# A hybrid attention layer: x given a second time by columns, and the first projection by feature chunks

## The reference

```python
u = rms_norm(h, attn_pre_g)                 # h = x, 512 x 1024
proj = u @ w_in                             # w_in 1024 x 1952
c_q, c_kv, k_r = proj[:, :256], proj[:, 256:384], proj[:, 384:416]
moba_qkv = proj[:, 416:]                    # 3 x 8 heads x 64
...                                         # two attention groups of 8 heads
h = h + rms_norm(mix @ w_out, attn_post_g)
u = rms_norm(h, mlp_pre_g)
h = h + rms_norm(square(relu(u @ w_up)) @ w_down, mlp_post_g)
```

## Time and profile before

| | |
|---|---|
| median of 3 runs | 570.49 us (570.36 to 570.64) |
| the profiled execution | 570.74 us |
| its span, first to last instruction | 568.9 us |
| PE busy | 553.5 us, 97% of the span |
| DVE, ACT, POOL busy | 392.3, 297.1, 95.2 us |
| mean granted TensorE clock | 0.997 |

### The profile page before, as it was taken

One profiled execution on the slowest core, in us unless ns is written; L12 is line 12 of the kernel. 1 busy time (PEld: TensorE's weight loads), 2 busy tenths in 40 slices (PEclk: granted clock), 3 DMA queues, 4 the chain that ended last, 5 costly groups with the idle time before them and its releaser, 6 DMA issues.

```text
span 568.9 us, 8013 instructions
## 1 busy us (share of the span) xinstructions
PE 553.5 (97%) x2824; PEld 460.6 (81%) x2824; DVE 392.3 (69%) x750; ACT 297.1 (52%) x624; POOL 95.2 (17%) x157
## 2 busy tenths in 40 slices
PE   7999999999999999999999999999999999999995
PEld 6988898877666788998888888888888888888883
DVE  3539572477885436537676677569868889787897
ACT  5573153588897353535434433435445657556461
POOL 1064020254779002200000000000000001000003
PEclk9999999999999999999999999999999999999998
DMA  8451242000002661078867788678985645506403
GB/s 298 153 149 56 88 172 75 0 2 2 0 2 75 236 191 55 1 296 279 292 241 253 280 258 298 238 251 294 337 297 189 221 162 209 199 24 221 149 1 148
DMA packets 42911, 95.15 MB, mean 167 GB/s; under 512 B 3840, under 2 KB 22016, under 8 KB 39552
## 3 DMA queue, kind: packets, MB, share of 16 engines
q1 hardware_dynamic: 41840, 94.74, 47.8%
q10 hardware_dynamic: 1040, 0.00, 0.1%
HBM read 79.01 MB, written 15.73 MB: 167 GB/s over the span
## 4 chain that ended last, share of the span: by engine, by line
PE 93%; ACT 2%; DVE 2%; DMA 1%; issue 1%; SPq 0%; POOLq 0%; DVEq 0%; POOL 0%; ACTq 0%
PE bank L1346 28%; PE bank L1347 28%; PE bank L1348 28%; PE bank L1550 2%; PE bank L1571 2%; PE bank L1512 1%; ACT probs L662 1%; DMA x_sb<-in_x 1%; DVE bank L1013 1%; PE bank L1456 1%; PE bank L1352 1%; PE bank L1385 1%; DVE pT L1062 0%; ACT pT L690 0%; PE bank L1475 0%
## 5 line engine op out<-in xcount | busy, mean ns | idle before, releaser
L1346 PE MATMUL bank<-uT_hi,w_hi 128*128 128x512 f32 (+1 forms) x280 | 104.1, 372 | 0.0
L1347 PE MATMUL bank<-uT_lo,w_hi 128*128 128x512 f32 (+1 forms) x280 | 103.9, 371 | 0.0
L1348 PE MATMUL bank<-uT_hi,w_lo 128*128 128x512 f32 (+1 forms) x280 | 103.8, 371 | 0.0
L1346 PE MATMUL bank<-w_hi,a_hi 128*128 128x512 f32 x224 | 87.3, 390 | 0.0
L1347 PE MATMUL bank<-w_lo,a_hi 128*128 128x512 f32 x224 | 87.2, 389 | 0.0
L1348 PE MATMUL bank<-w_hi,a_lo 128*128 128x512 f32 x224 | 87.2, 389 | 0.0
L893 DVE SCALAR_TENSOR_TENSOR w_lo<-w_raw,g_up,w_hi 128x256 fp32r<-128x256 f32 x128 | 52.1, 478 | 47.1 <-ACT w_hi L557 47.1
L557 ACT ACTIVATE w_hi<-w_raw,g_up 128x256 fp32r<-128x256 f32 x128 | 53.0, 496 | 44.7 <-PE bank L1348 28.5
L557 ACT ACTIVATE w_hi<-w_raw 128x1024 fp32r<-128x1024 f32 (+2 forms) x49 | 46.8, 1001 | 52.5 <-PE bank L1348 48.9
L890 DVE TENSOR_TENSOR w_lo<-w_raw,w_hi 128x1024 fp32r<-128x1024 f32 (+1 forms) x41 | 48.9, 1234 | 23.2 <-ACT w_hi L557 23.1
L1346 PE MATMUL bank<-w_hi,uT_hi 128*128 128x512 f32 (+1 forms) x160 | 62.1, 388 | 0.0
(11 more groups left out here) (157 smaller groups left out, 949.1 us busy)
## 6 DMA issues: line engine op xcount, KB each, us to landing
stage<-in_w_down SPq DMA_DIRECT2D x17, 1024.0 KB, 5.0
w_raw<-in_w_up SPq DMA_DIRECT2D x16, 1024.0 KB, 8.2
pair_sums<-stage SPq DMA_DIRECT2D x13, 1024.0 KB, 9.9
w_raw<-in_w_down SPq DMA_DIRECT2D x10, 1024.0 KB, 6.9
w_raw<-pair_sums SPq DMA_DIRECT2D x10, 1024.0 KB, 4.7
w_raw<-in_w_in SPq DMA_DIRECT2D x6, 1024.0 KB, 5.8
w_raw<-in_w_out SPq DMA_DIRECT2D x4, 1024.0 KB, 4.8
stage<-pair_sums SPq DMA_DIRECT2D x3, 1024.0 KB, 4.8
```

Source lines behind the costliest of these rows:

```text
L1346: nc.tensor.matmul(out, lh, rh, start=start, stop=False)
L1347: nc.tensor.matmul(out, lh, rl, start=False, stop=False)
L1348: return nc.tensor.matmul(out, ll, rh, start=False, stop=stop)
```

## The change

- x is given a second time, transposed on the host (`x_cols`, features by tokens). Its eight chunks of 128 features by 512 tokens go to a tile `x_raw`, and ACT and DVE split them straight from there. No tile of x is transposed on PE; x in its first layout is still loaded, for the norm, later.
- Group 0 goes by feature chunk: for each k all four tiles t, three matmuls each, in four PSUM banks that stay open over all eight chunks. Chunk 0 goes pass by pass over the tiles, the others tile by tile.
- ACT splits for each k first x, then the weights; DVE first the weights, then x. The weights of group 0 come as eight loads of 208 KB, each with its own semaphore.
- ACT's queue issues the chunks 0 and 1 of x and `g_in` between them; SP issues the rest, weights and x in turn. Both gains (`attn_pre_g`, `mlp_pre_g`) are laid out on the host as the tiles want them.
- One warming block of 20 matmuls in place of 12 and 24.

```diff
+    x_cols_v = x_cols.rearrange("(k p) t -> k p t", p=P)
...
+        with ExitStack() as cols:
+            x_raw = sb("x_raw", [P, ND, S], stack=cols)
...
+        def in_rows(k, by_row, by_chunk):
+            return (by_chunk, k // 4 + 1) if k % 4 == 3 else (by_row, k - k // 4 + 1)
...
-            x_half(0, 0)
-            for i, n in ((0, first_in), (1, raw_in[0])):
-                sp.dma_start(raw[0][:, 2 * CA * i:2 * CA * (i + 1)].rearrange("p (k n) -> p k n", k=2),
-                             w_in_v[:, 2 * i:2 * i + 2, 0:CA]).then_inc(n, 16)
-            for t in range(1, NT):
-                x_half(t, 0)
-            x_half(0, 1)
-            in_chunk(1)
-            for t in range(1, NT):
-                x_half(t, 1)
+            def first_rows(k):
+                w = slice(CA * (k % 4), CA * (k % 4) + CA)
+                sp.dma_start(raw[k // 4][:, w], w_in_v[:, k, 0:CA]).then_inc(raw_in[k // 4] if k % 4 == 3 else first_in[k], 16)
+
+            for k in range(ND):
+                first_rows(k)
+                if k >= 1 and k + 1 < ND:
+                    sp.dma_start(x_raw[:, k + 1, :], x_cols_v[k + 1]).then_inc(x_cols_in[k + 1], 16)
+            in_chunk(2)
+            for t in range(NT):
+                sp.dma_start(x_sb[:, t, :], x_v[t]).then_inc(x_in[t], 16)
...
-            for i in range(2, 6):
+            for i in range(3, 6):
                 in_chunk(i)
-            sp.dma_start(g_up[:, :], mlp_pre_g[0].rearrange("(k p) -> p k", p=P), allow_slow_non_contiguous=True).then_inc(g_up_in, 16)
+            sp.dma_start(g_up[:, :], mlp_pre_g).then_inc(g_up_in, 16)
...
-            act.dma_start(g_in[:, :], attn_pre_g[0].rearrange("(k p) -> p k", p=P), allow_slow_non_contiguous=True).then_inc(g_in_in, 16)
+            act.dma_start(x_raw[:, 0, :], x_cols_v[0]).then_inc(x_cols_in[0], 16)
+            act.dma_start(g_in[:, :], attn_pre_g).then_inc(g_in_in, 16)
+            act.dma_start(x_raw[:, 1, :], x_cols_v[1]).then_inc(x_cols_in[1], 16)
...
+            def first_hi(k):
+
+                act.wait_ge(x_cols_in[k], 16)
+                hi_part(uT_hi[:, k, :], x_raw[:, k, :]).then_inc(uh, 1)
+                if k == 0:
+                    act.wait_ge(g_in_in, 16)
+                act.wait_ge(*((raw_in[k // 4] if k % 4 == 3 else first_in[k]), 16))
+                w = slice(CA * (k % 4), CA * (k % 4) + CA)
+                hi_part(w_hi[w_slot(k // 4)][:, w], raw[k // 4][:, w], g_in[:, k:k + 1]).then_inc(in_rows(k, first_h, wh_ready)[0], 1)
...
+            for k in range(ND):
+                first_hi(k)
             in_hi(2)
             for t in range(NT):
-                for b in range(2):
-                    act.wait_ge(x_in[t][b], 16)
+                act.wait_ge(x_in[t], 16)
                 square(x_sb[:, t, :], 0, t, 0)
...
+            def first_lo(k):
+                dve.wait_ge(*in_rows(k, first_h, wh_ready))
+                w, s = slice(CA * (k % 4), CA * (k % 4) + CA), w_slot(k // 4)
+                lo_scaled(w_lo[s][:, w], raw[k // 4][:, w], g_in[:, k:k + 1], w_hi[s][:, w]).then_inc(in_rows(k, first_ready, w_ready)[0], 1)
+                dve.wait_ge(uh, k + 1)
+                lo_part(uT_lo[:, k, :], x_raw[:, k, :], uT_hi[:, k, :]).then_inc(ul, 1)
...
+            def first_group():
+
+                for k in range(ND):
+                    s, w = w_slot(k // 4), slice(CA * (k % 4), CA * (k % 4) + CA)
+                    passes = ((uT_hi, w_hi), (uT_hi, w_lo), (uT_lo, w_hi))
+                    if k == 0:
+                        pe.wait_ge(first_h, 1)
+                        pe.wait_ge(uh, 1)
+                        order = [(t, n) for n in range(3) for t in range(NT)]
+                    else:
+                        pe.wait_ge(*in_rows(k, first_ready, w_ready))
+                        pe.wait_ge(ul, k + 1)
+                        order = [(t, n) for t in range(NT) for n in range(3)]
+                    for t, n in order:
+                        if k == 0 and t == 0 and n >= 1:
+                            pe.wait_ge(first_ready if n == 1 else ul, 1)
+                        x, h = passes[n]
+                        last = nc.tensor.matmul(ps[t][:, 0:CA], x[:, k, P * t:P * t + P], h[s][:, w],
+                                                start=k == 0 and n == 0, stop=k == ND - 1 and n == 2)
+                        if k == ND - 1 and n == 2:
+                            last.then_inc(proj, 1)
+                    if k == 3:
+                        last.then_inc(w_used, 1)
...
             pe.wait_ge(consts, 3)
-            warm(12)
-            group(0, before_latents)
+            warm(20)
+            first_group()
             group(1, lambda part, t: None)
...
+    arrays["x_cols"] = np.ascontiguousarray(arrays["x"][0].T)
+    for name in ("attn_pre_g", "mlp_pre_g"):
+        arrays[name] = np.ascontiguousarray(arrays[name][0].reshape(-1, P).T)
```

More of the change, by code:

```diff
@@ L33, in build @@
 def build(nc, x, attn_pre_g, w_in, mla_q_norm_g, w_mla_q_up, mla_kv_norm_g, w_mla_kv_up, w_out,
-          attn_post_g, mlp_pre_g, w_up, w_down, mlp_post_g, rope_table, out):
+          attn_post_g, mlp_pre_g, w_up, w_down, mlp_post_g, rope_table, x_cols, out):
     S, D = x.shape[1], x.shape[2]
@@ L166, in build @@
         ps = [ctx.enter_context(nc.psum_tensor(f"bank{b}", [P, TOP], F32)) for b in range(8)]
-        x_in = [[sem(f"x{t}{b}_in") for b in "lr"] for t in range(NT)]
+        x_in = [sem(f"x{t}_in") for t in range(NT)]
+        x_cols_in = [sem(f"x_cols{k}_in") for k in range(ND)]
         h_in = [sem(f"h{t}_in") for t in range(NT)]
@@ L173, in build @@
         raw_in = [sem(f"raw{i}_in") for i in range(2)]
-        first_in = sem("first_in")
+        first_in = [sem(f"first{k}_in") for k in range(ND)]
         first_h, first_ready = sem("first_h"), sem("first_ready")
@@ L561, in in_hi @@
                 r, n = IN_CH[i], GROUP_COLS[i // 2][1]
[L562 to L565, removed]
+                arrived(r)
                 for k in range(4):
[L567 to L570, removed]
                     w, kg = slice(n * k, n * k + n), 4 * (i % 2) + k
@@ L583, in square, with transposed_hi @@
                                      accum_out=stat[:, norm, t, col:col + 1]).then_inc(sq, 1)
[L585 removed]
+            def transposed_hi(t):
                 for b in range(2):
[L588 removed]
+                    act.wait_ge(uT_full, 2 * t + b + 1)
                     hi_part(uT_hi[:, 4 * b:4 * b + 4, P * t:P * t + P],
                             ps[2 * t + b][:, :].rearrange("p (k n) -> p k n", k=4)).then_inc(uh, 1)
[L592 to L608, removed]
+            for k in range(ND):
+                first_hi(k)
             in_hi(2)
             for t in range(NT):
[L611 to L612 removed]
+                act.wait_ge(x_in[t], 16)
                 square(x_sb[:, t, :], 0, t, 0)
@@ L792, in _ @@
                 if t >= 1:
-                    transposed_hi(2 * NT, t - 1)
+                    transposed_hi(t - 1)
                 if t >= 2:
@@ L796, in _ @@
             square(h_sb[:, NT - 2, :], 4, NT - 2, 0)
-            transposed_hi(2 * NT, NT - 1)
+            transposed_hi(NT - 1)
             square(h_sb[:, NT - 1, :], 4, NT - 1, 0)
@@ L897, in in_lo @@
                 r, n = IN_CH[i], GROUP_COLS[i // 2][1]
-                dve.wait_ge(*((first_h, 1) if i == 0 else (wh_ready, r + 1)))
+                dve.wait_ge(wh_ready, r + 1)
                 for k in range(4):
-                    if i == 0 and k >= 1:
-                        last.then_inc(first_ready, 1)
-                        dve.wait_ge(*((first_h, k + 1) if k < 3 else (wh_ready, 1)))
                     w, kg = slice(n * k, n * k + n), 4 * (i % 2) + k
@@ L911, in transposed_lo @@
                     lo_part(uT_lo[sl], ps[2 * t + b][:, :].rearrange("p (k n) -> p k n", k=4), uT_hi[sl]).then_inc(ul, 1)
[L913 to L927, removed]
+            for k in range(ND):
+                first_lo(k)
             in_lo(2)
@@ L1364, in group @@
                         if t == 0:
-                            pe.wait_ge(*((first_ready, 1) if r == 0 else (w_ready, r + 1)))
+                            pe.wait_ge(w_ready, r + 1)
                         tok = slice(P * t, P * t + P)
                         for k in range(4):
-                            if r == 0 and t == 0 and k >= 1:
-                                pe.wait_ge(*((first_ready, k + 1) if k < 3 else (w_ready, 1)))
                             w = slice(n * k, n * k + n)
-                            last = mm3(ps[4 * (g > 0) + t][:, 0:n], uT_hi[:, 4 * part + k, tok], uT_lo[:, 4 * part + k, tok],
+                            last = mm3(ps[4 + t][:, 0:n], uT_hi[:, 4 * part + k, tok], uT_lo[:, 4 * part + k, tok],
                                        w_hi[w_slot(r)][:, w], w_lo[w_slot(r)][:, w], part == 0 and k == 0, part == 1 and k == 3)
@@ L1376, in group @@
                         last.then_inc(w_used, 1)
[L1378 to L1386, removed]
```

3 lines of the change are left out of this document (removed).

## The result

The changed kernel takes 566.79 us (median of 4 runs, 566.40 to 567.10) against 570.49: ratio 0.9935, 95% interval 0.9923 to 0.9947, or 3.7 us faster. The forecast was 565.6, within 564.3 to 568.2.

What follows compares the result with a forecast made beforehand. PE's own work was taken to bound the kernel; group 0 ending at 24.6 instead of 29.46 saves 4.9 us, so 570.74 becomes 565.9, less 0.25 for the median gives 565.6, range 564.3 to 568.2.

Steps and rivals of the forecast that it cites:

- Transposes removed: Group 0 on PE: 28 transposes of x amid its matmuls go away, sparing 2.7 us.
- The start: Before group 0: x chunk 0 lands at 4.4, ACT splits x and weights by 5.7, PE starts at 5.75.
- I take 4.4: Landing of x chunk 0: 524,000 bytes at 266 GB/s from 1.9, plus 0.5 us to the semaphore.
- T1: Moment PE starts chunk 1 of group 0, put at 8.7; 7.7 to 10.1 with landings at the bounds.
- B: Rival, chance 0.35: at the start PE's clock rises late after shorter warming and a gap; middle 567.0 us.
- Its first price: Late clock in chunk 0: 9 matmuls at 1.2 GHz by 8.85, chunk 0 ends 9.45, losing 0.8 us: 566.4.
- its second price: Late clock in group 0: 18 matmuls at 1.2 GHz by 11.95, group 0 ends at 26.7: 567.7 us.
- A: Whole kernel, chance 0.48: the forecast sum holds, 565.6 us; 564.6 to 567.0 with landings at the bounds.
- The rest of group 0: Chunk 1 to group 1: PE is slowest, waits no more, 84 matmuls take 15.9 us, ending at 24.6.
- What moves behind: Later weight chunks, norm loads and squares still arrive in time; weight chunk 2 has 3.8 us of cover; cost nothing.
- From group 1 on nothing differs: From group 1 on only a small gain load on SP differs, which nobody waited for; cost nothing.
- Absolute time: Sign of being wrong: group 1 starts earlier but the end does not follow, something behind it going by absolute time.

Runs made afterwards that it cites:

- the first profile: First profiled execution of the changed kernel, no further edit; execution 567.10 us, median 566.79 us.
- the second profile: Changed kernel run and profiled again, no edit; profiled execution 567.85 us, median 566.96 us.
- one queue: Changed kernel with all x and weight loads on SP's queue in order of use, only the gain on ACT's; 567.58 us.
- the transposes-back kernel: Changed kernel plus 28 transposes of the identity into idle banks, four behind each feature chunk from the second on; 570.75 us.
- the other order: Changed kernel with 30 warming matmuls, weights 0 and gain on ACT's queue, x 0, x 1, weights 1 and so on on SP's; 568.25 us.
- before with `w_up` early: Kernel before the change, with SP issuing `w_up` ahead of the wait for the store's end in the up projection; 570.41 us.

## Why the prediction was right, by its steps

The first point below needs two rows of PE's timeline in before, the transposes ahead of group 0:

```profile
3.91 1.06 PE L1385 MATMUL bank<-ident,x_sb 128*128 128x128 f32 x4
...
8.16 0.66 PE L1385 MATMUL bank<-ident,x_sb 128*128 128x128 f32 x4 [1.47 <-DMA x_sb<-in_x]
```

- **Transposes removed, 2.7 us.** Right in size, wrong in count: eight of the 32, not four, start before group 0's first matmul at 8.58, so 24 lay in its midst. The 2.72 us were read as a remainder and hold for whatever number it was, 0.113 us each with 24; the 28 put back cost 2.9 in the profile, 0.104 each.
- **The start.** x was ready at 4.38 for the 4.4 forecast and PE began at 5.85 for 5.75, but by another chain: the forecast had the gain for free, and it was the gain, landed at 5.1, that ended last, 0.15 us behind x's split. "I take 4.4" rested on 266 GB/s from 1.9 us; the rows show 111 until 2.5 and 319 to 391 from there on. These are two errors that cancel, so the hit is in part luck. Chunk 1 of x landed at 6.9 for 6.1, which put chunk 1's readiness at 9.3 for 8.7: the step counted only 256 KB of SP's beside it, but SP's chunk 2 of x, issued at 1.64, landed ahead of it, at 6.65.
- **T1.** 10.04 for 8.7: 0.6 us from chunk 1 of x, 0.7 from the clock. Of the rivals this is B: its place and mechanism are right, chunk 0 at 0.347 us a matmul. Its first price, 0.8 us, is near the clock's 0.7 in the first profile, but it had the rise at 8.85, and it came at 9.9; its second price had the rise at 11.95 and group 1 at 26.7, and the second profile has them at 11.8 and 26.67. The likeliest case A was not what happened. Its number was within 1.2 us, and the range held because its bounds for the landings reached to T1 = 10.1 and it made room for B.
- **The rest of group 0.** 15.85 us for 15.9, no wait, the split instructions at 0.63 and 0.68 for 0.60 and 0.69. The interleaving of the banks cost nothing, as forecast, but not for the reason given: the 0.189 us are no pace of one load, since they grow with the columns, to 0.23 for 512 (29.46 to 29.69 in before), each some 0.017 above columns at 2.4 GHz.
- **What moves behind.** Right in sign, its cover thinner than forecast: chunk 2 of the weights was split by 20.66 + 2.74 = 23.4, not 20.8, since its transfer, issued 11.09, was there only at 18; 2.5 us of cover in place of 3.8. Chunk 3 landed at 28.0 for "by 23", and the squares ended at 25.4 for 22; both still came before they were needed.
- **The second queue.** Taken as given, without a price against one queue. It had one: with one queue PE starts about 1.0 us earlier.
- **"From group 1 on nothing differs."** Right for this kernel, within 0.1 us in both profiles, but the prediction did not see how near the edge it was: the variants that started 0.9 to 1.6 us earlier still ran into the transfers of the up projection. "Absolute time" was not it either: the transfers move with group 1, but in steps longer than PE's.

The sum over these: forecast 4.9 us, found 3.57 in the profile and 3.7 in the medians; the 1.3 us between the forecast and the profile are T1's, the one term that was mis-sized. Still open: why the runs of the transposes-back kernel and of the other order lose up to 2 and 4 us more than their profiles show. That it is the same phase is likely for the latter, whose up projection took 164.2 us in the profile where 162.9 is usual, but its early-`w_up` version was not run.

## What to carry to other kernels

A gain at the start is worth its full size only while every later stage has slack against its own transfers: compare the step of each transfer chain with PE's step, not only the waits, which read zero until the slack is gone: here 11.74 us against 10.88 cost nothing in before and after, and 0.3 to 2.0 us in the profiles whose group 1 started 0.9 to 1.6 us sooner. A wait for a store in a queue that also feeds the bottleneck belongs behind the feeding load. And warming work is worth something when it lasts until the real work begins; here a break of 0.6 us was enough to lose it.

## What the runs showed of the hardware

- **The clock.** With PE working without a break from 2.67 us, its pace rose at 5.7 to 7.7 us (before, and five variants); in before with `w_up` early, with one break of 0.43 us at 7.5, at 7.3 to 8.7. With a break of 0.6 to 2.4 us before the real work it rose at 9.0 to 11.8 (after twice, and five variants), and 4 warming matmuls did as well as 20. The granted clock in the rows stood at 1.00 in all of them, while the pace was 0.107 us for 128 columns or 0.347 for 416; at the start only the distance of the matmuls tells the level. The Trainium skill ("TensorE: Matmul & The Clock Gate", Part 1) warns that clock events in a trace can be unreliable; these traces agree.
- **Two queues.** The first 256 KB of x landed 2.6 us after its issue from one queue, 3.4 to 3.6 with a second queue loading beside it, and 4.1 behind the gain on that second queue. The Trainium skill ("DMA: Bandwidth & Descriptors", Issuing engines are not separate DMA queues) says that transfers from several engines interleave on the same DMA engines and only issue time is saved. Here the weights were issued 0.44 us sooner, and x landed 1.0 us later.
- **A 4 KB load by single elements**, under way beside the others, went with a fall of the whole rate to a third for a microsecond (148 and 109 GB/s against 347 and 380 without it) and made the kernel 1.4 to 1.6 us slower in the medians.
